# Expert gather in features 0-3, 4-5, 6-7, and GpSimd in place of VectorE for the lower part of x's second tile

## The reference, cut to what matters

```python
g_logits = hf @ w_rg + b_rg                       # 4 groups: the best one is taken
_, g_idx = lax.top_k(g_logits, 1)
e_logits = (hf @ w_re + b_re).reshape(N, 4, 8)    # 8 experts a group
e_in_group = take_along_axis(e_logits, g_idx[:, :, None], axis=1)[:, 0]
top_v, top_i = lax.top_k(e_in_group, 2)           # the two best experts of that group
...
for g in range(N_GROUPS):
    act = silu(einsum('nd,edf->nef', h, w_gate[sl])) * einsum('nd,edf->nef', h, w_up[sl])
    act = act * combine[:, g, :, None]
    y = y + einsum('nef,efd->nd', act, w_down[sl])
```

## Time and profile before

| | us |
|---|---|
| median of 3 runs | 688.09 (688.09 to 688.76) |
| the profiled execution | 688.36 |
| its span in the profile | 686.5 |
| mean granted TensorE clock | 0.969 |
| TensorE busy | 637.4 (93%) |
| VectorE busy | 335.8 (49%) |
| ScalarE busy | 254.3 (37%) |
| GpSimd busy | 35.8 (5%) |
| transfers | 185.98 MB, mean 271 GB/s |

### The profile page before, as it was taken

One profiled execution on the slowest core, in us unless ns is written; L12 is line 12 of the kernel. 1 busy time (PEld: TensorE's weight loads), 2 busy tenths in 40 slices (PEclk: granted clock), 3 DMA queues, 4 the chain that ended last, 5 costly groups with the idle time before them and its releaser, 6 DMA issues.

```text
span 686.5 us, 10094 instructions
## 1 busy us (share of the span) xinstructions
PE 637.4 (93%) x4255; PEld 495.2 (72%) x4255; DVE 335.8 (49%) x409; ACT 254.3 (37%) x314; POOL 35.8 (5%) x25
## 2 busy tenths in 40 slices
PE   6999999999989988658868999999999999999995
PEld 5888999888856655335535588778888888888884
DVE  6856559656551121001111467678857444444436
ACT  6656563534411111000110454777234333433331
POOL 0010000000100000000000000742100000000002
PEclk9999999999999999957988999999999999999998
DMA  8979536688999999999999999335535555751001
GB/s 318 408 203 406 186 124 210 218 314 310 395 361 406 415 419 420 421 419 418 422 413 406 393 406 394 130 102 206 183 123 184 183 184 184 244 183 61 0 0 61
DMA packets 96358, 185.98 MB, mean 271 GB/s; under 512 B 9664, under 2 KB 33600, under 8 KB 96320
## 3 DMA queue, kind: packets, MB, share of 16 engines
q1 hardware_dynamic: 96032, 185.36, 72.0%
q10 hardware_dynamic: 288, 0.07, 0.0%
HBM read 184.37 MB, written 1.05 MB: 270 GB/s over the span
## 4 chain that ended last, share of the span: by engine, by line
PE 84%; DMA 8%; DVE 4%; issue 2%; ACT 1%; SPq 1%; POOL 0%; DVEq 0%; ACTq 0%
PE ps L721 20%; PE ps L723 20%; PE ps L722 20%; DMA ring<-in_w_down_e 5%; PE ps L977 4%; PE ps L1051 3%; PE ps L1006 3%; PE ps L1084 3%; PE ps L1072 2%; PE ps L1021 2%; DMA ring<-in_w_up_e 2%; DMA ring<-in_w_in 1%; PE ps L1372 1%; DVE heT L2267 1%; SPq L530 1%
## 5 line engine op out<-in xcount | busy, mean ns | idle before, releaser
L1481 ACT ACTIVATE w_hi<-ring 128x2048 fp32r<-128x2048 f32 (+1 forms) x65 | 117.1, 1828 | 12.6 <-PE ps L723 7.5
L1947 DVE TENSOR_TENSOR w_lo<-ring,w_hi 128x2048 fp32r<-128x2048 f32 x43 | 97.8, 2286 | 22.5 <-ACT w_hi L1481 22.3
L722 PE MATMUL ps<-w_lo,xT_hi 128*128 128x512 f32 (+1 forms) x272 | 102.6, 377 | 0.0
L721 PE MATMUL ps<-w_hi,xT_hi 128*128 128x512 f32 x240 | 96.0, 400 | 0.5 <-DVE xT_lo L2362 0.3
L723 PE MATMUL ps<-w_hi,xT_lo 128*128 128x512 f32 x240 | 93.7, 391 | 0.0
L722 PEld LDWEIGHTS ps<-w_lo,xT_hi 128*128 128x128 f32 x272 | 51.3, 189 | 8.7
L721 PEld LDWEIGHTS ps<-w_hi,xT_hi 128*128 128x128 f32 x240 | 45.1, 188 | 10.8 <-issue 0.8
L723 PEld LDWEIGHTS ps<-w_hi,xT_lo 128*128 128x128 f32 x240 | 45.0, 188 | 9.8
L721 PE MATMUL ps<-w_hi,hR_hi 128*128 128x512 f32 x112 | 44.3, 395 | 0.2 <-DVE w_lo L1979 0.2
L723 PE MATMUL ps<-w_hi,hR_lo 128*128 128x512 f32 x112 | 43.6, 390 | 0.0
L722 PE MATMUL ps<-w_lo,hR_hi 128*128 128x512 f32 x112 | 43.6, 389 | 0.0
(11 more groups left out here) (349 smaller groups left out, 1195.7 us busy)
## 6 DMA issues: line engine op xcount, KB each, us to landing
ring<-in_w_in SPq DMA_DIRECT2D x28, 1024.0 KB, 13.4
ring<-in_w_up_e SPq DMA_DIRECT2D x28, 1024.0 KB, 14.6
ring<-in_w_gate_e SPq DMA_DIRECT2D x27, 1024.0 KB, 12.2
ring<-in_w_down_e SPq DMA_DIRECT2D x24, 1024.0 KB, 17.8
ring<-in_w_gate SPq DMA_DIRECT2D x11, 1024.0 KB, 5.2
ring<-in_w_up SPq DMA_DIRECT2D x11, 1024.0 KB, 7.4
ring<-in_w_down SPq DMA_DIRECT2D x11, 1024.0 KB, 5.0
ring<-in_w_out SPq DMA_DIRECT2D x8, 1024.0 KB, 9.8
```

The costliest lines, as they stand in the source:

```text
L721: mm(o, a_hi, b_hi, start=start, stop=False, skip_group_check=True)
L722: mm(o, a_hi, b_lo, start=False, stop=False, skip_group_check=True)
L1481: return nc.scalar.activation(o, i, ACT.Copy)
L1947: tt(w_lo[slot][:], ring[:, slot, :], f32(upper_of(i)), ALU.subtract).then_inc(lo_made, 1)
```

## The change

Two things are changed. Each group's gather is cut in three calls in place of two: feature tiles 0 to 3, 4 and 5, and, after unit 0 as before, 6 and 7. And the lower part of x's second tile is made by GpSimd, after that of the first tile, and no longer by VectorE; xslo_made is then raised once for each of the three results by GpSimd alone.

```diff
@@ quad_hidden @@
                 pe.wait_ge(s["pick_made"], it * 2 + 1)
                 pe.wait_ge(s["y_made"], it * 2 + 1)
-                gather(range(0, 6), s, waits)
+                gather(range(0, 4), s, waits)
+                gather(range(4, 6), s, waits)
                 pe.wait_ge(s["turned_made"], it * 2 + 1)
@@ VectorE, after slots(0, start0, 1) @@
-            dve.wait_ge(xshi_made, T)
-            dve.wait_ge(xslo_made, 1)
-            for dst, ks in ((xs_lo1a, slice(0, KD // 2)), (xs_lo1b, slice(KD // 2, KD))):
-                x = X[:, 1, :].rearrange("p (q k) -> p k q", k=KD)
-                tt(dst[:], x[:, ks, :], f32(xs_hi[:, 1, ks, :]), ALU.subtract).then_inc(xslo_made, 1)
@@ GpSimd, xs_lower @@
                 for dst, ks in parts:
-                    ins = tt(dst[:], x[:, ks, :], xs_hi[:, t, ks, :].bitcast(F32), ALU.subtract)
-                ins.then_inc(xslo_made, 1)
+                    tt(dst[:], x[:, ks, :], xs_hi[:, t, ks, :].bitcast(F32), ALU.subtract).then_inc(xslo_made, 1)
 
             xs_lower(0, ((xs_lo0, slice(0, KD)),))
+            xs_lower(1, ((xs_lo1a, slice(0, KD // 2)), (xs_lo1b, slice(KD // 2, KD))))
```

## The result

The changed kernel is slower: its median is 692.79 us (688.70 to 694.67, 17 runs) against 688.45 (687.32 to 690.30, 17 runs) of the kernel before on the same chips, a ratio of 1.0043 with an interval of 1.0028 to 1.0058. Two of the 97 times of the kernel before in this document, both over 800 us, are left out everywhere.

The account below looks back on a forecast made before the run. Weight transfers were taken to bound the expert groups: 2.35 us of router delay less 0.66 us gather gain put the refill and the end 1.69 us later, 689.8 us against a median of 688.09, range 687.2 to 691.2.

Parts of the forecast that it names:

- The port: Router before the gather: GpSimd's two subtractions each hold up a VectorE instruction, making pick 2.35 us late; chance 0.60.
- The gather: Three-part gather lets heT start sooner: 0.66 us gained in group 0, nothing booked for the other seven groups.
- The refill: SP's first refill of the weight ring, after unit 0: issued 1.69 us later, at 197.9 instead of 196.23.
- From the refill to the end: Groups 0 to 7: the refill's 1.69 us delay passes in full to all landings and the end.
- had an idle road in front: Start of the weight stream: early_c and the refill, landing in 7.8 and 7.9 us, met no queue.
- that rule: Groups 0 to 7: only what moves the start of the full transfer stream counts, and it counts once.
- rival D: Longer TensorE idle time before the gather drops its clock; 2.1 us more before the refill, 691.9 us; chance 0.08.
- the engine was fully busy ahead of it: Reason given against a clock drop in TensorE's longer idle time, from 189.8 to about 192.8 us.
- my own bound: Whole kernel: a difference up to 0.2% (1.38 us) counts as no change.

Follow-up runs that it names:

- pool_late: Changed kernel, but GpSimd's two halves for the second tile wait until VectorE has done the router; 1.0019 of the kernel before.
- gather_only: Kernel before with only the gather cut in three; VectorE keeps the second tile's lower part; 0.9984 of the kernel before, 1.0004 when repeated.
- pool_only_fill: Kernel before with GpSimd making the second tile's lower part, plus 16 constant matmuls in TensorE's idle time before the rank matmuls; 1.0018 of the kernel before.
- pool_only: Kernel before with only the second tile's lower part moved to GpSimd, gather as before; 1.0101 of the kernel before.
- after_again: The changed kernel run again without edit; 1.0047 of the kernel before, profiled execution 693.40 us at half clock.
- fill_router: Changed kernel plus 16 matmuls on constants in TensorE's idle time before the rank matmuls; 1.0001 of the kernel before.
- dve_early: Kernel before with three-part gather and VectorE's two subtractions moved right behind the logits, GpSimd making tile 0 alone; 1.0077 of the kernel before.
- half_pool: Three-part gather; GpSimd makes only the first half of the second tile's lower part, VectorE the other after pick; 1.0004 of the kernel before.

## Why the prediction was wrong

**The port.** Right, to 0.03 us in the sum: the two router rows and their position, and the delay (1.06 + 1.29 us foreseen, 1.14 + 1.25 measured), pick 2.38 us late against 2.35. The Trainium skill's rule of an exclusive lock ("SBUF — State Buffer", section "SBUF: two separate sides") is borne out by these rows, and by 1.53 and 1.50 us in pool_late; that the lock is held for the whole instruction is not quite so, as VectorE's rows end 0.04 and 0.06 us behind GpSimd's here, and an operation of 0.19 us must have started before that end.

**The gather.** Right: 0.66 us in group 0, nothing that can be told from groups 1 to 7 (gather_only: 0.9984 and 1.0004).

**The refill.** Right: 1.71 us later against 1.69 forecast.

**From the refill to the end.** Wrong by 1.0 us. I held that the stream moves with the refill one for one, since both transfers "had an idle road in front", on the ground that they took 7.8 and 7.9 us. The transfers issued in 193 to 200 us of the changed kernel show otherwise (KB each, us to landing):

```profile
early_c<-in_w_up_e SPq DMA_DIRECT2D x1, 1024.0 KB, 7.9
ring<-in_w_gate_e SPq DMA_DIRECT2D x1, 1024.0 KB, 6.6
```

With 3.9 us between them and not 2.4, the refill lands in 6.6 us; in pool_only_fill, pool_only and after_again, issued 4.6 to 7.0 us behind early_c, it lands in 4.8 to 4.9. So up to 3 of its 7.9 us before were waiting behind what was under way, and the road was not idle. The stream's start hung on early_c as well as on the refill (pool_late), and about 1 us of refill delay was free: 1.71 later gave a lag of 0.70, 2.40 gave 1.33, 1.72 gave 0.51, and 0.67 earlier gave nothing. Where this 1 us goes is argued from these lags, not traced. The second half of that rule held: once the stream is full, the lag is carried unchanged through 56 MB and more, and counts once.

**The clock.** This is the step that failed. I had it as rival D, at a chance of 0.08 and a price of 2.1 us. It happens in 16 of 29 executions of the changed kernel, if those over 692.5 us are counted (two of the 29 have a trace, one of either kind), and the price in the stream is 4.85 - 0.70 = 4.15 us, which the times bear out: the first 17 runs' upper part lies 4.1 us over the lower one by the means. My reason against it, that "the engine was fully busy ahead of it", was worth nothing: the same busy stretch stands ahead of the hole in after_again. The price was short because I counted the gather and unit 0 (2.1 us; measured 2.63 to the refill) and not the refills behind it, whose units are also used at half clock, 2.2 us over the four. Added up: 0.7 us always, 4.15 us in a little over half of the executions, is 3.0 us on average; measured 0.43% of 688.45 is 3.0 us. The median of 692.79 is one of the upper part, and outside my range of 687.2 to 691.2. The direction, slower by over 0.2%, was given 0.55 and came, but by luck: 0.47 of it stood on the held router alone, and with the clock kept up this gives a lag of 0.5 to 0.7 us and a ratio of 1.0001 (fill_router), no change by my own bound. What made the kernel slower is the step that had 0.08.

That the loss follows from the idle time is shown by the fill (the times over 692.5 us go, with GpSimd's work as it was), and dve_early supports it (such times come without that work, their clock untraced). What decides from one execution to the next whether it falls after the same 2.98 us of idle time is open.

## What to carry to other kernels

Before work is put on an idle GpSimd, look at what VectorE does at that time, not at whether GpSimd has time: here a chain of 0.2 us operations on the critical path lost 1.14 and 1.25 us to two GpSimd subtractions of 1.5 us each. Price a longer wait of TensorE ahead of a start-up phase with the clock in mind, count all the work that runs at half clock before the next buffer is full, and look at the spread of many executions before one profile is believed: here the profile of the changed kernel shows 0.6 us of a loss of 3. Where a wait can't be shortened, matmuls on constants in TensorE's idle time can help: here they took away all of the loss that can be told (1.0001), though they made nothing faster than before the change.

## What the runs showed that I had not expected

TensorE went to 1.2 GHz behind a wait of only 1.74 us in a busy stretch (half_pool's profiled execution; a second of the 12 has such a time), and full work did not bring the clock back at once: in after_again all of 196 to 204 us, with TensorE busy throughout, ran at 0.50. Not only VectorE operations with two tensor inputs were held: in pool_late a TENSOR_SCALAR of 128x16 with one took 1.50 us instead of 0.18 beside GpSimd's subtraction. GpSimd's subtraction of 128x512 took 1.51 us where it shut VectorE out, 1.79 and 1.58 in pool_late, where it started beside a VectorE instruction of that kind. And a 1 MB transfer that was issued with 2.4 us to the one ahead took 7.9 us, with 3.9 us 6.6, with 4.6 to 7.0 us 4.8 to 4.9.
